# Attention scores of two packs in one step, with the low key products on 64 rows of the array each

## The reference, cut to what matters

```python
sc  = einsum('bgpqd,bgnd->bgpqn', q, k_cmp)    # compressed branch, 31 keys
ss  = einsum('bgpqd,bgqnld->bgpqnl', q, k_sel) # selected blocks
sw  = einsum('bgpqd,bgkd->bgpqk', q, k_win)    # sliding window of 512
p   = softmax(where(valid, score, NEG_INF))    # each branch
o   = gate0 * p_c @ v_c + gate1 * p_s @ v_s + gate2 * p_w @ v_w
```

## Time and profile before

| | |
|---|---|
| median of 3 runs | 2392.85 us (2390.38 to 2394.16) |
| the profiled execution | 2390.76 us |
| its span, first to last instruction | 2388.4 us |
| mean granted TensorE clock | 0.999 |
| TensorE products, loads busy | 2377.3, 2008.9 us |
| VectorE, ScalarE busy | 1334.7, 900.6 us |
| attention with its value projection, first layer | from 131 to 319 us |
| the same, second attention layer | from 1793 to 1980 us |

### The profile page before, as it was taken

The page is one execution under the profiler, slowest core; times in us unless marked ns, Lnnn a source line. Parts: engine busy times, 40 slices in busy tenths (PEclk is TensorE's granted clock), DMA queues, the critical chain, the costliest instruction groups (busy, mean ns, idle before and its releaser), DMA issues.

```text
span 2388.4 us, 33645 instructions
## 1 busy us (share of the span) xinstructions
PE 2377.3 (100%) x11808; PEld 2008.9 (84%) x11808; DVE 1334.7 (56%) x2198; ACT 900.6 (38%) x1374; POOL 308.5 (13%) x305
## 2 busy tenths in 40 slices
PE   9999999999999999999999999999999999999998
PEld 8889988888888888888888888888889998888887
DVE  8667765444465664343587644446766675534444
ACT  6267743222233432222333322223426783322223
POOL 2211140000030120000033000003421114000003
PEclk9999999999999999999999999999999999999999
DMA  4810013232333232322233223233560002223232
GB/s 157 222 54 2 2 62 106 88 106 88 106 106 106 89 106 88 106 97 97 93 101 105 98 89 104 89 105 106 136 191 27 2 2 88 97 88 106 88 104 90
DMA packets 64472, 220.56 MB, mean 92 GB/s; under 512 B 7664, under 2 KB 7792, under 8 KB 64368
## 3 DMA queue, kind: packets, MB, share of 16 engines
q1 hardware_dynamic: 58608, 209.09, 26.4%
q0 software_dynamic: 5184, 8.40, 1.7%
q10 hardware_dynamic: 576, 1.69, 0.2%
HBM read 208.65 MB, written 2.10 MB: 88 GB/s over the span
## 4 chain that ended last, share of the span: by engine, by line
PE 98%; DVE 1%; DMA 0%; issue 0%; ACT 0%; DVEq 0%; SPq 0%
PE bank L1479 95%; PE bank L1736 3%; DMA raw<-stream 0%; PE bank L1766 0%; DVE branch L1247 0%; DVE attn L1209 0%; DVE branch L1262 0%; DVE big L1472 0%; DVE nmax L1212 0%; DVE attn L1215 0%; DVE rden L1242 0%; ACT L579 0%; DVE rden L1244 0%; ACT w_hi L563 0%; DVE rden L1259 0%
## 5 line engine op out<-in xcount | busy, mean ns | idle before, releaser
L1479 PE MATMUL bank<-xs_hi,w_hi 128*128 128x512 f32 x1808 | 708.4, 392 | 0.5 <-DVE work L1093 0.4
L1479 PE MATMUL bank<-xs_hi,w_lo 128*128 128x512 f32 x1808 | 703.6, 389 | 0.0
L1479 PE MATMUL bank<-xs_lo,w_hi 128*128 128x512 f32 x1808 | 703.5, 389 | 0.0
L915 DVE TENSOR_TENSOR w_lo<-raw,w_hi 128x1024 fp32r<-128x1024 f32 x372 | 473.2, 1275 | 236.8 <-ACT w_hi L563 232.5
L563 ACT ACTIVATE w_hi<-raw 128x1024 fp32r<-128x1024 f32 x373 | 391.9, 1051 | 444.8 <-PE bank L1479 239.5
L1479 PEld LDWEIGHTS bank<-xs_hi,w_hi 128*128 128x128 f32 x1808 | 339.4, 188 | 72.0 <-issue 2.2
L1479 PEld LDWEIGHTS bank<-xs_lo,w_hi 128*128 128x128 f32 x1808 | 339.4, 188 | 70.9 <-issue 1.0
L1479 PEld LDWEIGHTS bank<-xs_hi,w_lo 128*128 128x128 f32 x1808 | 339.3, 188 | 70.8
L1479 PE MATMUL bank<-hid_hi,w_hi 128*128 128x512 f32 x720 | 280.6, 390 | 0.0
L1479 PE MATMUL bank<-hid_lo,w_hi 128*128 128x512 f32 x720 | 280.1, 389 | 0.0
L1479 PE MATMUL bank<-hid_hi,w_lo 128*128 128x512 f32 x720 | 280.1, 389 | 0.0
(11 more groups left out here) (206 smaller groups left out, 2719.6 us busy)
## 6 DMA issues: line engine op xcount, KB each, us to landing
raw<-stream SPq DMA_DIRECT2D x371, 512.0 KB, 3.2
w_f<-stream SPq DMA_DIRECT2D x18, 512.0 KB, 3.8
hid_hi<-mix_hi POOLq DMA_DIRECT2D x32, 128.0 KB, 6.6
hid_lo<-mix_hi POOLq DMA_DIRECT2D x32, 128.0 KB, 6.6
x<-x_in SPq DMA_DIRECT2D x8, 256.0 KB, 8.5
out<-big SPq DMA_DIRECT2D x8, 256.0 KB, 2.7
raw<-stream ACTq DMA_DIRECT2D x2, 512.0 KB, 7.6
big<-consts SPq DMA_DIRECT2D x1, 640.0 KB, 9.7
```

What stands on the lines that cost most here:

```text
L915: nc.vector.tensor_tensor(w_lo[:, slot, :], raw[:, k, :], f32(w_hi[:, slot, :]), ALU.subtract).then_inc(w_lo_ready, counted(b))
L1479: return nc.tensor.matmul(out_, w, v, start=start, stop=stop)
```

## The change

At t = 1, 2 and 3 the packs are taken in pairs, and the scores of both are made in one step, the first of the two. First come the products with `key_hi` of both packs, on 128 rows. Then come the products with `key_lo`, on 64 rows each: for an even head rows 0 to 63, for an odd head rows 64 to 127, that is the rows that hold the high part of the query. They go alternately to the two packs' banks. The product of the low query part with the low key part is left out. In the second step of a pair TensorE makes no scores. The wait ahead of a pair is for `max_ready` of `p0 + p`: the maximum of pack p - 1 must be taken too. At t = 1 a pack now holds two even or two odd heads instead of two neighbours. The compressed packs and t = 0 stay as they were, and so do the programs of VectorE and ScalarE except for the order of heads at t = 1.

```diff
+SIDE_BY_SIDE = 1
@@ units(p)
+    if t_of(i) == 1:
+        return [((r - 1) // 4, r // 2 % 2 + 2 * k) for k in range(n)]
     return [((r + k - 1) // 4, (r + k - 1) % 4) for k in range(n)]
+
+def with_next(p):
+    i, r, n = PACKS[p]
+    return r > 0 and t_of(i) >= SIDE_BY_SIDE and (r - 1) // n % 2 == 0
@@ attention, TensorE
+                def scores_of_two(p):
+                    i = PACKS[p][0]
+                    g, t = i // TT, t_of(i)
+                    w = P * (t + 1)
+                    pe.wait_ge(max_ready, p0 + p)
+                    for d in range(2):
+                        for k, (br, j) in enumerate(units(p + d)):
+                            mm(bank[score_bank(l0, p + d)][:, bass.ts(k, w)], q_home[g][:, j, bass.ts(t, P)],
+                               key_hi[:, br, g, 0:w], k == 0, False)
+                    for k in range(PACKS[p][2]):
+                        for d in range(2):
+                            br, j = units(p + d)[k]
+                            rows = slice(64 * (j % 2), 64 * (j % 2) + 64)
+                            last = mm(bank[score_bank(l0, p + d)][:, bass.ts(k, w)], q_home[g][rows, j, bass.ts(t, P)],
+                                      key_lo[rows, br, g, 0:w], False, k == PACKS[p][2] - 1)
+                            if k == PACKS[p][2] - 1:
+                                last.then_inc(score_ready, 1)
@@ steps(lo, hi)
-                        if s < NPACKS:
+                        if s < NPACKS and with_next(s):
+                            scores_of_two(s)
+                        elif s < NPACKS and not (s and with_next(s - 1)):
                             scores(s)
```

## The result

The changed kernel takes 2439.8 us as a median of 6 runs (2438.7 to 2443.0) against 2391.0 for the kernel before: ratio 1.020, interval 1.019 to 1.021, or 48.8 us more. The forecast was slower by 39, at 2432. The profiled execution has a span of 2437.1 us, and its mean granted TensorE clock is 0.994 where it was 0.999. Of all executions told of in this document one, of e7, took 2964.7 us at a granted clock of 0.752 and is left out of e7's median.

What follows compares the result with a forecast made beforehand. TensorE's program was taken to bound the kernel. From 2390.8 us, + 15.9 (holds) + 22.7 (waits) - 12.4 (side by side) + 12.8 (changes of form) = + 39.0 gave 2429.8, as a median 2432; range 2406 to 2456.

Steps and rivals of the forecast that it cites:

- holds at the heads: Each attention layer's head: TensorE waits for VectorE's maxima of packs 0 and 2, 3.75 and 4.2 us; + 15.9 us.
- rival 3: TensorE's clock falls in the holds at the layer heads, 2.2 us four times: + 8.8 us, 2441; chance 0.08.
- waits inside the items: Inside attention items, TensorE waits for VectorE's maxima before pairs: 11.35 us a layer, + 22.7 us, bounds 11 and 28.
- changes of form: In pair steps, switching between 128 and 64 rows costs 0.1 us each, counted for 128 changes: + 12.8 us.
- side by side: In a pair's scores, four streams become three: 7.1 us at t = 3, 5.3 at t = 2; - 12.4 us.
- upper bound of 0.28: Most that one change between 128 and 64 rows could cost: 0.171 us of tail plus a 0.112 us load.
- 32 changes swallowed by waits: Of 160 changes, some 32 back to 128 rows stand before a new wait and cost nothing, leaving 128.
- a sign that the prediction itself named: The prediction is wrong if the waits inside the items are under 10 us in the profile after.
- 1.6 an item forecast: At t = 1, TensorE is held 0.5 us before an item's first pair and 1.1 before its second.
- 0.95 and 0.8: Waits at t = 2 (0.2, 0.5 and 0.25 us) and at t = 3 (0.2 and 0.6 us).
- given them back only once: From t = 0 to t = 3, existing waits offset most of a 0.6 us hold, leaving 0.2, three times.
- start of the count: Median of the earlier kernel's runs shown, 2392.9 us, 2.1 above the profiled run's 2390.8; the forecast was counted from it.

Runs made afterwards that it cites:

- e7: The changed kernel with pairs only at t = 3, the head of a layer one by one, low products on 64 rows: 2391.9 us, ratio 1.000.
- e10: The changed kernel with 17 products of ones ahead of each of the two waits at a layer's head, keeping TensorE busy: 2430.1 us, ratio 1.016.
- e1: The changed kernel with packs 1 to 4 of each layer made one by one, all other pairs kept: 2412.6 us, ratio 1.009.
- e3: The changed kernel with low key products on all 128 rows and packs 1 to 4 of a layer one by one: 2402.4 us, ratio 1.005.
- e8: e1 with both low products of a pair on rows 0 to 63, so they can't run side by side: 2425.9 us, ratio 1.014.
- e4: The kernel before, without pairs or new wait, its single low key product at t = 2 and t = 3 on 64 rows: 2430.3 us, ratio 1.017.
- e6: e1 with VectorE's low queries of t = 0 items one step later, behind the second pack's maximum at t = 1: 2407.9 us, ratio 1.007.
- e12: The kernel before with pairs at t = 2 and 3 on 128 rows, head one by one, the pair's wait parted: 2386.3 us, ratio 0.9980.

## Why the prediction was right in direction and range, term by term

| term | forecast | measured | from |
|---|---|---|---|
| holds at the heads | + 15.9 | + 17.5 | e10 less e1 |
| lower clock behind them | 0 (rival 3: + 8.8) | + 9.7 | after less e10 |
| waits inside the items | + 22.7 | + 11.9 | e3 less before |
| changes of form | + 12.8 | + 23.5 | e8 less e3 |
| side by side | - 12.4 | - 13.4 | e1 less e8 |
| sum | + 39.0 | + 49.2 | measured 48.8 |

The measured terms are differences of runs that form a chain from the kernel before to the changed one, so their sum must give the whole and proves nothing about the single terms; 49.2 is not 48.8 only because e3's series has another median of the kernel before.

The holds were read right. VectorE's program order fixed both: TensorE was to go on at 137.88 and did at 137.90, though the first product record shows the engine idle for only 3.48 us, since the record before it has a tail. Second hold: from the value block's last product to the restart 4.53 forecast, 4.49 measured (145.94 to 150.43).

The clock was named as a rival at 0.08 with 2.2 us a hold, and it came: 2.4 a hold on average. It had to be in the forecast, not beside it. No row of before has TensorE idle so long, so the rows could not decide it. The Trainium skill, "TensorE: Matmul & The Clock Gate", Part 1 on the HAM clock gate, has the clock fall when TensorE idles. The trace agrees, with a granted clock of 0.50 after 4.0 us of idle time and 1.00 when the same 4.0 us are filled (e10), though after the very first hold it fell only 1.5 us behind the restart. That the price taken from the start of the kernel came close is luck: the granted clock reads 1.00 in that stretch, so the row shows slow instructions and not which level they ran at, and the single holds cost from 1.7 to some 3 us.

The changes of form were mis-sized: 0.15 us each for all 152 in e1 against 0.1 for 128. I took the price of one unhidden load. In the trace it is 0.09 going in, with the load no longer ahead of its product, and about 0.25 coming out, 0.19 to the first transpose and 0.06 behind it. The load is unhidden there too; what the rest is isn't shown. My upper bound of 0.28 was meant for each change and was too much. The Trainium skill, "TensorEngine Tiling (Array Packing)", Key Properties, says that changing the mode drains the engine. The spacings agree in part: the records, whose ends are modelled, overlap by 0.07 us at a change and by 0.16 to 0.17 elsewhere, so by them the engine isn't quite empty. Nor were 32 changes swallowed by waits: e4, which has no new waits, has nearly the same price for each.

The waits inside the items were over-counted by half. By a sign that the prediction itself named this term failed: waits in the items under 10 us. The profile has 7.2 us of them where about 23 were foretold. A record's tail hides up to 0.2 us of each of the twenty (the first hold is recorded with 3.48 us where the starts are 3.71 apart), and e3's 11.9 us of time lie above 10, but not by much. At t = 1 they came out nearly as counted: 1.6 an item forecast (0.5 and 1.1), 1.40 in e3; 0.6 forecast in the first group, 0.55 in e3; and e6 shows the queries as the cause of 0.85 of it. At t = 2 and t = 3 I forecast 0.95 and 0.8; e3 has + 0.27 and - 0.34. Two things were missing in TensorE's count. The two products of the compressed pack (260 columns) are 0.22 us apart, not one slot of 0.11:

```profile
219.97 0.60 PE L1488 MATMUL bank<-vbd_all,attn 128*128 128x260 f32 x2
220.42 0.49 PE L1765 MATMUL bank<-ident,attn 128*128 128x128 f32 x3
```

And at t = 3 the two waits on the normalizations that the kernel before has the earlier trace rows, 0.4 us an item, are covered by the longer scores of a pair. I had seen those and given them back only once. The first makes 0.33 us, of 0.68 too much at t = 2; both make some 0.7, of 1.1 too much at t = 3. The rest stays open, and no run isolates the two. The 0.3 at t = 0 was not foreseen at all. It comes with the pairs at t = 1: e4 and e12, which have none, show 5.36 and 5.37. Why isn't shown; my guess is that VectorE is late there with tasks of t = 1.

The side by side gain was right in sum, 12.4 against 13.4 (12.3 by the own series). By item, e8 less e1, t = 3 has 0.89 (4 x 0.22, as forecast), t = 2 0.41 (0.67 forecast) and t = 1 0.35, which I had at nothing; there loads bind, and the gain says that loads of two halves overlap too, as the load record at 203.44 shows for t = 3 (two in 0.19 us). Why t = 2 gives less I did not test; waits there may cover a part.

Direction came from the holds, which were read right. The closeness is luck: errors of + 9.7, + 10.7, + 1.6 stand against - 10.8 and - 1.0. Form and waits cancelled, and the clock is about what is left. That is also why rival 3, the forecast with the clock added, met the time at 2441: its terms for form and waits were as wrong. And the start of the count, 2392.9 from three runs, was 1.9 above the 2391.0 of six, so 2432 lies 7.8 us off while the difference, + 39.0 for + 48.8, is 9.8 off.

## What to carry to other kernels

A pair of half-height products must save more than two changes of form, here 0.31 us, before it is worth anything: 512 columns save 0.22, and e7 is the case at its best. Before two steps are merged, read in the other engine's program what stands between the two results that the merged step waits for, above all at the head of a stage, where the order is another one; and part the wait, so that work which needs less goes first. A hold of some 4 us can cost half as much again through TensorE's clock, here 9.7 us on 17.5.

## What the runs showed of the hardware that I had not expected

- Going from 128 to 64 rows costs 0.09 us and coming back some 0.25, and by the time of whole kernels it is 0.15 a change, in two of different build (e4, and e8 with e3). At both changes the weight load starts with its product and not 0.2 us ahead of it.
- After 3.5 us of idle TensorE the granted clock stayed at 1.00 for 1.5 us more in one layer and then was 0.50 until 4.9 us after the restart; in the other layer, and after 4.0 us, it fell during the idle time. Products came at 0.43 us instead of 0.23 up to 5.8 us after a restart (150.43 to 156.21).
- A product of ones in f32 with 128 columns is two instructions of 0.11 us, so a filler must be counted in instructions.
- Two low products on different halves start within 0.01 us of each other, as foretold, but where loads bind (t = 1) they gain too, 0.35 us an item; on the same half they take a full stream more (0.66 in place of 0.43).
